# Seven block products for tiles 14 to 21 of both down projections, pairs 0 and 1 interleaved

## The reference

```
def swiglu(h, w_gate, w_up, w_down):
    return (jax.nn.silu(h @ w_gate) * (h @ w_up)) @ w_down
...
    h = h + swiglu(rms_norm(h, ffn_norm[i]), ffn_w_gate[i], ffn_w_up[i], ffn_w_down[i])
return rms_norm(h, final_norm)
```

## Time and profile before

| | us |
|---|---|
| median of three runs | 1063.45 |
| profiled execution, its whole time | 1061.74 |
| its span | 1060.0 |
| TensorE busy | 1051.7 (99%) |
| VectorE busy | 846.2 (80%) |
| ScalarE busy | 529.2 (50%) |

### The profile page before, as it was taken

How to read it: one execution, slowest core, us unless ns; L and a number is a source line. 1 busy time by engine, 2 the same in 40 slices (tenths; PEclk the granted TensorE clock), 3 DMA queues, 4 the chain that set the end, 5 groups by cost and what they waited for, 6 DMA issues and landing times.

```text
span 1060.0 us, 17801 instructions
## 1 busy us (share of the span) xinstructions
PE 1051.7 (99%) x6766; PEld 954.8 (90%) x6766; DVE 846.2 (80%) x1195; ACT 529.2 (50%) x755; POOL 41.8 (4%) x24
## 2 busy tenths in 40 slices
PE   9999999999999999999999999999999999999998
PEld 8888888899999999888888888888999999988997
DVE  6777775999999998634678677689999999898675
ACT  6688873745554555421443323365445545563332
POOL 0232230000000000000000000000000000000000
PEclk9999999999999999999999999999999999999999
DMA  8121112233223323223223232222332233232212
GB/s 338 51 70 50 67 53 80 80 120 119 85 113 119 102 96 109 92 97 109 107 82 116 83 117 83 86 114 80 119 119 91 107 119 109 79 110 101 92 67 80
DMA packets 16967, 106.21 MB, mean 100 GB/s; under 512 B 1888, under 2 KB 2272, under 8 KB 6432
## 3 DMA queue, kind: packets, MB, share of 16 engines
q1 hardware_dynamic: 16560, 104.86, 27.5%
q10 hardware_dynamic: 288, 0.56, 0.2%
q0 software_dynamic: 80, 0.26, 0.1%
HBM read 103.59 MB, written 2.10 MB: 100 GB/s over the span
## 4 chain that ended last, share of the span: by engine, by line
PE 95%; DVE 2%; ACT 1%; issue 1%; DMA 0%; DVEq 0%
PE bank L502 31%; PE bank L503 31%; PE bank L504 31%; PE bank L669 1%; ACT split L1228 1%; DMA first_raw<-weights_in 0%; PE bank L657 0%; PE bank L655 0%; DVE s_lo L1826 0%; PE bank L541 0%; PE bank L576 0%; DVE mid_lo L1510 0%; PE bank L911 0%; PE bank L923 0%; PE bank L555 0%
## 5 line engine op out<-in xcount | busy, mean ns | idle before, releaser
L502 PE MATMUL bank<-x_hi,split 128*128 128x256 f32 (+1 forms) x704 | 204.1, 290 | 0.0
L503 PE MATMUL bank<-x_lo,split 128*128 128x256 f32 (+1 forms) x704 | 203.4, 289 | 0.0
L504 PE MATMUL bank<-x_hi,split 128*128 128x256 f32 (+1 forms) x704 | 203.4, 289 | 0.0
L957 ACT ACTIVATE split<-raw 128x2048 fp32r<-128x2048 f32 (+2 forms) x51 | 90.1, 1766 | 136.2 <-PE bank L504 136.1
L1467 DVE TENSOR_TENSOR split<-raw,split 128x2048 fp32r<-128x2048 f32 (+2 forms) x43 | 92.5, 2152 | 59.2 <-ACT split L957 59.1
L502 PEld LDWEIGHTS bank<-x_hi,split 128*128 128x128 f32 x704 | 132.3, 188 | 3.0 <-issue 0.5
L503 PEld LDWEIGHTS bank<-x_lo,split 128*128 128x128 f32 x704 | 132.3, 188 | 3.0 <-issue 0.5
L502 PE MATMUL bank<-x_hi,s_hi 128*128 128x256 f32 x480 | 134.3, 280 | 0.6 <-ACT work L1238 0.6
L504 PEld LDWEIGHTS bank<-x_hi,split 128*128 128x128 f32 x704 | 132.3, 188 | 2.5
L503 PE MATMUL bank<-x_lo,s_hi 128*128 128x256 f32 x480 | 133.8, 279 | 0.0
L504 PE MATMUL bank<-x_hi,s_lo 128*128 128x256 f32 x480 | 133.8, 279 | 0.0
(11 more groups left out here) (280 smaller groups left out, 2209.4 us busy)
## 6 DMA issues: line engine op xcount, KB each, us to landing
raw<-weights_in SPq DMA_DIRECT2D x82, 1024.0 KB, 4.8
raw<-weights_in SPq DMA_DIRECT2D x12, 768.0 KB, 4.2
work<-x SPq DMA_DIRECT2D x4, 512.0 KB, 12.6
raw<-weights_in SPq DMA_DIRECT2D x4, 512.0 KB, 3.7
out<-head SPq DMA_DIRECT2D x3, 512.0 KB, 2.7
head<-head_in SPq DMA_DIRECT2D x1, 768.0 KB, 9.0
first_raw<-weights_in SPq DMA_DIRECT2D x3, 192.0 KB, 5.1
first_raw<-weights_in SPq DMA_DIRECT2D x1, 576.0 KB, 7.7
```

The lines of the kernel that those rows point to most:

```text
L502: pe.matmul(o, lhs[0], rhs[0], start=start, stop=False, skip_group_check=True)
L503: pe.matmul(o, lhs[0], rhs[1], start=False, stop=False, skip_group_check=True)
L504: return pe.matmul(o, lhs[1], rhs[0], start=False, stop=stop, skip_group_check=True)
L957: act.activation(w_hi[s][:, 0:n], raw[s][:, 0:n], ACT.Copy).then_inc(hi_split[s], 1)
```

## The change

Both down projections now run the same list (`DOWN_ORDER`): part 0 of pair 0, part 1 of pair 0, part 0 of pair 1, part 2 of pair 0, parts 1 and 2 of pair 1, then parts 0, 2, 1 of pair 2 and of pair 3. Part 2 is tiles 14 to 21. It is seven block products for pairs 0, 1 and 2 in layer 1 (pair 3's is plain) and for all four pairs in layer 2. TensorE's first block product waits for all low parts of the inner activation and of the tail forms. The loop of layer 1 is written out. The convolution's operands are prepared in a new order among these parts, and two of their buffers trade places. In the first round of each feed-forward, ScalarE now makes both copies of the `up` product before it splits the next chunk's blocks. The unchanged end of layer 2 (`last_pair`) keeps its order. The diff, cut to its core:

```diff
@@ -48,14 +48,13 @@
 HALF = ROPE // 2
 SLOT = KD * 2 * P
 PAIRS = HEADS // 2
-DOWN_K = [range(0, 8), range(8, 16), range(16, KF)]
 UQ_N = KQ * 2 * (NOPE + ROPE)
 UKV_N = KKV * 2 * (NOPE + VDIM)
-DOWN_N = [len(ks) * 2 * P for ks in DOWN_K]
-DOWN_AHEAD = (DOWN_N * 3)[2:8]
 LAST_K = [range(0, 8), range(8, 14), range(14, KF)]
-LAST_ORDER = [(0, 1, 2)] * 2 + [(0, 2, 1)] * 2
-LAST_N = [len(LAST_K[i]) * 2 * P for order in LAST_ORDER for i in order]
+PARTS_FIRST = [(0, 0), (0, 1), (1, 0), (0, 2), (1, 1), (1, 2), (2, 0), (2, 2), (2, 1)]
+DOWN_ORDER = [PARTS_FIRST + [(3, 0), (3, 2), (3, 1)]] * 2
+PART_N = [len(ks) * 2 * P for ks in LAST_K]
+DOWN_SIZES = [[PART_N[i] for _, i in order] for order in DOWN_ORDER]
...
@@ -406,11 +405,11 @@
             c = loads(c, 2, [SLOT] * 2)
             for layer in range(2):
                 c = loads(c, KF // 2, [SLOT] * 2)
+                for k, n in enumerate(DOWN_SIZES[layer]):
+                    load(k % 2, c + k, n)
+                c += len(DOWN_SIZES[layer])
                 if layer == 0:
-                    c = loads(c, 2, DOWN_N * 2)
                     c = loads(c, 8, [SLOT] * 2)
-            for k, n in enumerate(LAST_N):
-                load(k % 2, c + k, n)
             for j in range(TOK - 1):
                 sp.wait_ge(left_ready, j + 1)
...
@@ -845,39 +844,26 @@
                     winograd(0, GATE_BANK)
                     winograd(1, UP_BANK)
...
+                plain0, plain1 = DOWN_BANKS
+                chunk(0, plain0, INNER, LAST_K[0], True, False, ready=made)
+                last_tiles(1, plain0, LAST_K[1], made)
+                chunk(0, plain1, INNER, LAST_K[0], True, False)
+                pe.wait_ge(operand_ready, made + KF)
+                pe.wait_ge(inner_split, T.add("inner_forms", K_PAIRS))
+                winograd(1, 0, inner_block, DOWN_SUMS)
+                last_tiles(0, plain1, LAST_K[1])
+                winograd(1, 0, inner_block, DOWN_SUMS)
+                chunk(0, plain0, INNER, LAST_K[0], True, False)
+                winograd(1, 0, inner_block, DOWN_SUMS)
+                last_tiles(0, plain0, LAST_K[1])
                 if last:
-                    banks = DOWN_BANKS[0]
...
-                    last_pair(1, DOWN_BANKS[1][0], LAST_K[1], True)
+                    last_pair(1, plain1[0], LAST_K[1], True)
                 else:
-                    with T.loop(pe, 2, slot0=3, slot1=3, b4=1, b5=1, b6=1, b7=1):
-                        for c in range(6):
-                            down_chunk(c)
+                    chunk(1, plain1, INNER, LAST_K[0], True, False)
+                    chunk(0, plain1, INNER, LAST_K[2], False, False)
+                    last_tiles(1, plain1, LAST_K[1])
                 return made + KF
...
                 copy_last(0, 0)
-            def up():
+            def up(copy_first=False):
+                if copy_first:
+                    copy(1, 1)
                 blocks_hi(0)
-                copy(1, 1)
+                copy(1, 5 if copy_first else 1)
                 sums_hi_of(0)
-                copy(1, 5)
+                if not copy_first:
+                    copy(1, 5)
                 silu(0)
...
-            def last_down():
+            def down(layer):
                 split(0)
-                split(1)
                 for k in range(K_PAIRS):
                     cols = slice(k * 2 * SEQ, (k + 1) * 2 * SEQ)
-                    act.wait_ge(inner_formed, k + 1)
+                    act.wait_ge(inner_formed, layer * K_PAIRS + k + 1)
                     act.activation(inner_tail_hi[:, cols], inner_tail[:, cols], ACT.Copy).then_inc(inner_tail_high, 1)
-                split(0, LAST_N[1])
+                block_forms_hi(1)
+                split(0, PART_N[1])
+                down_copies_of(1)
+                block_forms_hi(1)
                 pair_squares(0)
-                block_forms_hi(1)
                 split(0)
                 down_copies_of(1)
                 block_forms_hi(1)
                 pair_squares(1)
-                split(0, LAST_N[1])
+                split(0, PART_N[1])
                 down_copies_of(1)
                 split(1)
+                if layer:
+                    last_pair()
+                else:
+                    conv_operands()
...
+            def conv_operands():
+                split(0)
+                pair_squares(2)
+                split(1, PART_N[1])
+                for k in range(2):
+                    conv_scaled(k)
+                for k in range(2):
+                    conv_tail_hi(k)
+                split(0)
+                conv_scaled(2)
+                conv_tail_hi(2)
+                pair_squares(3)
+                split(1)
+                conv_scaled(3)
+                conv_tail_hi(3)
...
-            def done(s):
-                v.wait_ge(chunk_done[s], T.now(f"slot{s}"))
+            def done(s, before=0):
+                v.wait_ge(chunk_done[s], T.now(f"slot{s}") - before)
...
-                split(1, DOWN_N[1] if name else LAST_N[1])
-                if name:
-                    inner_rests(range(12, KF))
-                else:
-                    inner_rests(range(12, LAST_K[2][0]))
-                    for k in range(K_PAIRS):
-                        inner_forms(k, LAST_K[2][2 * k])
-                        if k == 1:
-                            split(0)
+                split(1, PART_N[1])
+                inner_rests(range(12, LAST_K[2][0]))
+                for k in range(K_PAIRS):
+                    inner_forms(k, LAST_K[2][2 * k])
+                    if k == 1:
+                        split(0)
...
+                def conv_operands():
+                    split(1)
+                    add_corners((4, 5), False)
                     settle()
+                    normed_pair(0)
                     split(0)
-                    v.wait_ge(sums_split[1], T.now("sums1"))
-                    forms(1)
-                    down_corners(1)
-                    forms_split(1, DOWN_SUMS)
-                    add_corners((2, 3), True)
-                    added()
-                    add_squares([tile(work, 4), tile(work, 5)])
-                    split(0, LAST_N[1])
-                    down_corners(1)
+                    normed_pair(1)
+                    pair_sums(DOWN_BANKS[0], (4, 5), 0, True, before=1)
+                    squares_of_pair()
+                    normed_pair(2)
+                    split(1, PART_N[1])
+                    for k in range(2):
+                        conv_forms(k)
+                    conv_tail_rest(0)
+                    split(0)
+                    conv_tail_rest(1)
+                    conv_forms(2)
+                    pair_sums(DOWN_BANKS[1], (6, 7), 1, True)
+                    normed_pair(3)
+                    squares_of_pair()
+                    split(1)
+                    conv_tail_rest(2)
+                    conv_forms(3)
...
@@ -2078,11 +2054,34 @@
                     weigh([KD - 2])
                     add_squares([tile(work, 4)])
+                def next_forms():
+                    v.wait_ge(sums_split[1], T.now("sums1"))
+                    forms(1)
+                forms(1)
+                for k in range(K_PAIRS):
+                    inner_tail_rest(k)
+                forms_split(1, DOWN_SUMS)
+                pair_sums(DOWN_BANKS[0], (0, 1), 1, False, before=1)
+                split(0, PART_N[1])
+                next_forms()
+                down_corners(1)
+                forms_split(1, DOWN_SUMS)
+                add_corners((0, 1), True)
+                squares_of_pair()
+                split(0)
+                next_forms()
+                pair_sums(DOWN_BANKS[1], (2, 3), 0, False, before=1)
+                down_corners(1)
+                forms_split(1, DOWN_SUMS)
+                add_corners((2, 3), True)
+                squares_of_pair()
+                split(0, PART_N[1])
+                down_corners(1)
                 if name:
-                    down_round(0)
-                    down_round(4)
+                    conv_operands()
                 else:
-                    last_down()
+                    last_pair()
             clear_acc()
...
-        for m in range(KD // 2):
-            for i in LAST_ORDER[m] if layer else range(3):
-                ks = (LAST_K if layer else DOWN_K)[i]
-                chunk = columns(w["ffn_w_down"][layer][ks[0] * P:(ks[-1] + 1) * P], span(m * 2 * P))
-                yield block_order(chunk) if layer and m and i == 2 else chunk
+        for m, i in DOWN_ORDER[layer]:
+            ks = LAST_K[i]
+            chunk = columns(w["ffn_w_down"][layer][ks[0] * P:(ks[-1] + 1) * P], span(m * 2 * P))
+            yield block_order(chunk) if i == 2 and (layer or m < K_PAIRS - 1) else chunk
```

(34 more changed lines are left out.)

70 lines of the change are left out of this document (9 added, 61 removed).

## The result

The changed kernel took 1068.02 us (median of 4 runs, 1067.62 to 1068.95), the kernel before 1062.73 beside it (1061.59 to 1063.56): a ratio of 1.0056, 95% interval 1.0044 to 1.0069. It is slower by more than the 0.2% that can be told from no change. The profiled execution took 1067.62 us, its span 1065.4.

A forecast was written before the change was run, and what follows sets the result against it. TensorE was taken as the bound, with VectorE slower at the head of a down projection. Columns -3.8, stall -0.35, waits +7.6 and copies +0.2 gave +3.65 us, a predicted median of 1067.1 us, range 1064.0 to 1069.5.

The forecast's parts named there:

- The head of the down projections: First block product, each layer: TensorE wants the blocks at 29.92 us, VectorE delivers late, a pause of 3.4 us.
- The second wait: After the first block product's opening part, each layer: TensorE waits for the sums' remainders, 0.2 us more.
- The columns and the stall: Down projections: four conversions to block products save 0.95 us each, 3.8 in all; layer 2's late plain part saves 0.35.
- Slow matmuls: Behind the pause in each down projection some matmuls come slower: 0.2 us a layer, at a clock of 1.00.
- third rival: The clock falls to half in the down projections' pauses: 2 us a layer, +4 in all, 1071 us; chance 0.08.
- copies' order: First up product of each feed-forward, copies ahead of the split: pause moves by one product, +0.1 us a layer.
- the two waits: Pause, second wait and slow matmuls at the first block product: 3.8 us a layer, 7.6 together.
- second rival: The copies' new order is worth its whole pause: -0.81 us in each layer instead of +0.1, 1065.3 us; chance 0.13.
- The sum: Whole kernel: -3.8 - 0.35 + 7.6 + 0.2 = +3.65 us, predicted median 1067.1 us.
- first rival: VectorE delivers the first product's blocks in time, only the columns count: -3.95 us, 1059.5 us; chance 0.07.

The follow-up runs named there:

- The kernel with the filled pause: Changed kernel plus twelve 512-column matmuls on ready operands ahead of TensorE's wait for the first block product, both layers: 1067.4 us, ratio 1.0036.
- the version without a pause: Changed kernel with part 1 of pair 1 moved ahead of the first block product, in both layers, and the other weight slot read: 1057.62 us, ratio 0.9945.
- the longer pause: Changed kernel plus one VectorE operation of 1.2 us on unused values ahead of the blocks' remainders, in each layer: 1071.71 us, ratio 1.0085.

## Why the prediction was right, point by point

**The head of the down projections.** Right, to some 0.1 us. TensorE reached the first block product 29.93 us after the start (451.14 - 421.21; 29.92 had been summed up), the blocks' remainders ended 33.26 after it (454.47 - 421.21; 964.91 - 931.65 = 33.26 had been). The pause was 3.53 us where 3.4 stood: VectorE's end takes 0.20 to TensorE's next matmul, and I had set 0.04. The order of operations on VectorE is the one summed up, and ScalarE's high parts were not in the way, though the kernel without tail remainders shows them only 2.0 us behind.

**The second wait.** TensorE's part ahead of the sums took 1.54 us (454.67 to 456.21) for 1.40 at full pace: 0.14 for the 0.2 forecast, of which 0.07 already lies behind the first matmul (454.67 to 454.86). The kernel with the filled pause shows what this wait and slow matmuls were worth together at the full clock: its down projection took 3.73 us more than the one without a pause (120.64 and 116.91), of which 3.55 lie between the filling's start and the block product (453.16 to 456.71). The 0.18 left stand against 0.4 in the forecast.

**The columns and the stall.** Right: 9.92 us for a block product, 2.81 for the three conversions of layer 1 in the version without a pause. The plain part that took 11.23 us is gone in layer 2, and with it its 0.35. VectorE's added work in layer 1's down projection was summed up as some 30 us and is 35.8 (99.94 for 64.16); it brought no further wait, as forecast: from 459.6 on no matmul of that stage comes more than 0.03 us late.

**Slow matmuls, and the third rival.** The forecast had 0.2 us a layer for matmuls that come slowly behind the pause and a clock of 1.00 throughout; the clock was the third rival, with 2 us a layer and a chance of 0.08. That was the larger of two steps that failed; the other is the copies' order, below. The clock did fall, behind both pauses; by the filled pause it cost 1.43 us a layer, 2.9 in all. I had argued that the array would stand for only some 3.1 us; it stood for 3.37, and 2.36 was enough in two of four cases. With 3.53 + 0.14 + 1.43 = 5.1 us a layer in place of 3.8 the two waits are worth 10.2, not 7.6; layer 1's down projection, forecast at 120.7 us, took 122.07. The rival's time of 1071 was too high, since the start of the kernel was the wrong row for the length of the slow stretch. The Trainium skill ("TensorE: Matmul & The Clock Gate", Why this matters for your kernels) warns of such a gap in the middle of a kernel. The runs agree for the pauses of the changed kernel, and show that a clearly shorter one is not safe: 2.35 to 2.39 us brought the fall in two of four cases, 1.25 us and less in none of four. I should have given this rival much more than 0.08: nothing in the trace spoke against it but a guess on the gap's length.

**The copies' order.** The size was wrong, and the sign: +0.1 a layer in the sum, -0.42 and -0.32 measured, -0.42 and -0.33 by itself in the kernel before. The pause at 239.28 is gone, as said. What failed is the start of ScalarE's split. The forecast had it behind both copies of the up product, from 237.9 on, and VectorE 0.48 us later for it; the description of the change says both copies too. The diff puts only the first copy ahead of the blocks' split; the second stands between it and the sums' split. ScalarE in the changed kernel:
```profile
236.22 0.39 ACT L1204 ACTIVATE work<-bank 128x256 f32<-128x256 f32 x1 [0.95 <-PE bank L503]
237.02 1.92 ACT L1194 ACTIVATE split<-raw 128x2048 fp32r<-128x2048 f32 x1 [0.41 <-DVE work L1810]
```
The copy is done before VectorE's form releases the split, which begins at 237.02 for 237.03 before. VectorE takes it up at 239.36 for 239.38, and nothing is pushed back. In the next product, a gate product, the copy expected near 249.1 is over at 248.60, for 248.62 before, and TensorE, 0.81 us earlier, wants it then:
```profile
248.50 0.28 PE L503 MATMUL bank<-x_hi,split 128*128 128x256 f32 x1
248.65 0.39 PE L501 MATMUL bank<-x_hi,s_hi 128*128 128x256 f32 x1
...
250.04 0.28 PE L503 MATMUL bank<-x_hi,s_lo 128*128 128x256 f32 x1
250.30 0.38 PE L501 MATMUL bank<-x_hi,s_hi 128*128 128x256 f32 x1
```
The matmul at 248.65 comes 0.03 us later than at the usual pace, and the one behind it 0.11 later. The one at 250.30 waits for the copy behind the sums (249.87 to 250.25): 0.14 late, and the one behind it 0.10. The forecast had 0.2 for this copy, which was right. These four spacings are the 0.39 us by which the product exceeds 9.80; all its others are at the usual pace. So of the old 0.81 the pause of 0.44 shrank to 0.03, and the rest moved by one product (0.35 us, for 0.4 in the forecast). The kernel was at the middle between the forecast and the second rival (-0.81).

**The sum.** Forecast, for the profile: -3.8 - 0.35 + 7.6 + 0.2 = +3.65. By the measured terms: -3.8 - 0.35 + 10.2 - 0.75 = +5.3, against 5.5 by stage. The predicted 1067.1 is 0.9 below the 1068.02 measured; the two errors, 2.6 us for the clock and 0.95 for the copies, have opposite signs and leave 1.65, of which 0.7 is covered by the median before, 1062.73 in these runs and 1063.45 in the ones I started from. So the direction and the two pauses were foreseen, but that the median came within 0.9 us is in part luck: a term left out and a term with the wrong sign cancelled. The range held the result. The first rival fell: VectorE does more in the idle part of its stage and still comes late at the head.

## What to carry to other kernels

When work is moved to an engine that looks idle, add up its queue at the place where the first result is wanted, from the operation rows: here it fixed a wait to 0.1 us, and moving one part of 8 us ahead of the wait turned +0.6% into -0.5%. Pauses of TensorE of 2.35 us and more in a full stream brought the half clock in eight of ten profiled cases here; such a pause is to be priced at its length and 1.4 to 1.5 us more, until a run shows otherwise. Where the pause can't go, matmuls on ready operands kept the clock here. Before pricing a new order, read it from the diff and not from its description: one copy taken for two cost a term its sign. Measure a change of tenths by stage in the profiles, not by medians alone, where a kernel's times lie in groups.

## What the runs showed of the hardware that was not expected

**The clock behind a pause.** Pauses of 3.35 to 3.38 us of the array brought the half clock (1.2 GHz) behind all four seen in two profiles of the changed kernel, 4.64 and 4.65 us behind both, 2.35 to 2.39 us behind two of four, 0.90 to 1.25 us behind none of four. It is not tied to the restart. In the first profile of the changed kernel it came on up to 1.4 us after it, in the second, at the same stage, 0.35 us after it (clock 1.00 from 454.82 to 455.10 and 0.50 from 455.20 on), and with the longer pause it was there before TensorE resumed. The first profile:
```profile
456.21:460.46 4.25, 4.25 (x24) 4.25 (x24) 4.18 (x6) 0.77 (x2) 0.00 (x0) 0.62 0.54 224
```
These 24 matmuls took 4.25 us, while the twelve ahead of them, right behind the pause, had come at the full pace from 454.67 on.

**Two paces at one clock.** The kernel before, profiled twice: layer 1's gate and up stretch in the first execution, and in the second.
```profile
226.23:421.64 195.41, 195.13 (x1670) 194.75 (x1669) 182.09 (x237) 102.30 (x143) 0.00 (x0) 1.00 0.30 108
```
```profile
226.40:423.53 197.13, 196.85 (x1671) 196.47 (x1669) 182.31 (x237) 102.41 (x143) 0.00 (x0) 1.00 0.30 107
```
The clock is 1.00 in both and TensorE idles for 0.28 us in both, but the second is 1.72 us longer. It doesn't start so: its first block product takes 9.80 us as well, and only behind the short stops of the first up product each takes 9.89 us, 117.8 ns a matmul for 116.7:
```profile
225.00:234.80 9.80, 9.80 (x85) 9.80 (x84) 8.05 (x10) 4.22 (x5) 0.00 (x0) 1.00 0.31 115
242.61:252.50 9.89, 9.89 (x86) 9.89 (x85) 9.38 (x13) 4.61 (x6) 0.00 (x0) 1.00 0.30 106
```
The 13 profiles hold 26 such stretches. All run at 116.7 ns up to their short stops; behind them 17 stay there, and 9 run at 117.8 ns to the end of the stretch. With the new order of copies the stops, and with them the slower pace, come one product later. That is why the times of one kernel lie in groups about 1.7 us apart (before: 1061.7, 1063.5, 1065.3; changed, in its second series: 1067.7, 1069.3, 1070.8; in its first two of four, 1068.3 and 1069.0, lie between), and why stages are compared here between profiles of the same pace. The down projections and the mixer have one pace alone (119.72 us in both profiles of before). All five runs of the fastest version fell within 0.2 us of each other, and nine of the twelve with the old copies within 0.4, the other three higher; with so few runs this can be chance, and the cause of the two paces is open.
